# Starting the mixer and the dense layer on token tile 0, and reordering the heads' projection and the first loads, in a two-layer hybrid decoder trunk

## What is computed

```python
h = rmsnorm(x, pre_mix_g[l])
z = h @ w_in[l]                        # 2560 columns: q, k, v (8 heads x 64), u, g (512 each)
attn = dilated_mixture_attention(rotary(q), rotary(k), v)
uc = causal_dwconv(u, conv_w[l], conv_b[l])
rec = gelu(g) * rg_lru(uc, ...)        # two sigmoid gates, exp, sqrt, a scan over tokens
mixed = concatenate([rmsnorm(attn), rmsnorm(rec)])
x = x + rmsnorm(mixed @ w_out[l], post_mix_g[l])
h = rmsnorm(x, pre_ffn_g[l])
f = swiglu(h, ...) if l == 0 else moe_ffn(h, ...)   # dense 3584 wide; 8 experts, 2 per token
x = x + rmsnorm(f, post_ffn_g[l])
```

## Time and profile before

| | us |
|---|---|
| median of three executions | 1459.18 |
| the profiled execution | 1459.41 |
| its span, first to last instruction | 1457.6 |
| PE busy in the span | 1439.0 (fillers included) |
| DVE, ACT busy | 1196.2, 1032.0 |
| share of PE in the chain that ended last | 94% |
| start, mixer and norms of layer 0 | until about 128 |
| dense layer | 128 to 363 |
| second mixer and norms | 363 to 485 |
| router and experts | 485 to the end |

### The profile page before, as it was taken

One profiled execution on the slowest core, in us unless ns is written; L12 is line 12 of the kernel. 1 busy time (PEld: TensorE's weight loads), 2 busy tenths in 40 slices (PEclk: granted clock), 3 DMA queues, 4 the chain that ended last, 5 costly groups with the idle time before them and its releaser, 6 DMA issues.

```text
span 1457.6 us, 20750 instructions
## 1 busy us (share of the span) xinstructions
PE 1439.0 (99%) x7076; PEld 1193.5 (82%) x7076; DVE 1196.2 (82%) x1378; ACT 1032.0 (71%) x1258; POOL 14.5 (1%) x13
## 2 busy tenths in 40 slices
PE   8999999999999999999999999999999999999997
PEld 7887888888887688888888888888888888888885
DVE  7867656555776798898899899989889889989997
ACT  7665445445565677787797787788778779778774
POOL 0000000000000200000000000000000000001000
PEclk9999999999999999999999999999999999999999
DMA  9525874554433399999999999999999999999991
GB/s 367 208 100 197 339 274 177 201 200 173 147 143 127 112 423 409 361 393 388 378 370 397 375 362 409 376 353 400 386 358 399 388 366 378 397 373 372 420 400 65
DMA packets 68611, 454.11 MB, mean 312 GB/s; under 512 B 9424, under 2 KB 9552, under 8 KB 16592
## 3 DMA queue, kind: packets, MB, share of 16 engines
q1 hardware_dynamic: 60768, 432.47, 76.6%
q10 hardware_dynamic: 6640, 16.78, 3.2%
q0 software_dynamic: 1152, 4.19, 0.7%
HBM read 438.21 MB, written 15.20 MB: 311 GB/s over the span
## 4 chain that ended last, share of the span: by engine, by line
PE 94%; DVE 3%; ACT 2%; issue 1%; DMA 0%; DVEq 0%; ACTq 0%
PE psum L472 26%; PE psum L474 26%; PE psum L473 26%; PE psum L760 7%; PE psum L763 4%; PE psum L822 2%; ACT lru_b L938 1%; PE psum L479 1%; DVE hn L1300 1%; DVE xs L1322 1%; DVE hn L1316 1%; PE psum L621 0%; PE psum L561 0%; PE psum L805 0%; PE psum L499 0%
## 5 line engine op out<-in xcount | busy, mean ns | idle before, releaser
L1211 DVE TENSOR_TENSOR w_lo<-ring,w_hi 128x1024 fp32r<-128x1024 f32 x812 | 941.0, 1219 | 57.1 <-ACT w_hi L925 56.4
L925 ACT ACTIVATE w_hi<-ring 128x1024 fp32r<-128x1024 f32 x812 | 807.5, 1053 | 56.1 <-PE psum L474 49.7
L472 PE MATMUL psum<-w_hi,hT_both 128*128 128x512 f32 (+1 forms) x1088 | 424.4, 390 | 1.4 <-DVE hT_both L1222 1.4
L474 PE MATMUL psum<-w_hi,hT_both 128*128 128x512 f32 (+1 forms) x1088 | 417.6, 384 | 0.0
L473 PE MATMUL psum<-w_lo,hT_both 128*128 128x512 f32 (+1 forms) x1088 | 416.8, 383 | 0.0
L474 PEld LDWEIGHTS psum<-w_hi,hT_both 128*128 128x128 f32 x1088 | 204.4, 188 | 41.1
L472 PEld LDWEIGHTS psum<-w_hi,hT_both 128*128 128x128 f32 x1088 | 204.6, 188 | 40.7 <-DVE hT_both L1222 1.8
L473 PEld LDWEIGHTS psum<-w_lo,hT_both 128*128 128x128 f32 x1088 | 204.8, 188 | 38.4 <-issue 0.2
L472 PE MATMUL psum<-w_hi,act_hi 128*128 128x512 f32 x560 | 218.9, 391 | 0.9 <-DVE act_lo L1222 0.9
L474 PE MATMUL psum<-w_hi,act_lo 128*128 128x512 f32 x560 | 218.2, 390 | 0.0
L473 PE MATMUL psum<-w_lo,act_hi 128*128 128x512 f32 x560 | 218.2, 390 | 0.0
(11 more groups left out here) (236 smaller groups left out, 898.5 us busy)
## 6 DMA issues: line engine op xcount, KB each, us to landing
ring<-moe_gate SPq DMA_DIRECT2D x112, 1024.0 KB, 7.2
ring<-moe_up SPq DMA_DIRECT2D x112, 1024.0 KB, 7.6
ring<-moe_down SPq DMA_DIRECT2D x112, 1024.0 KB, 7.3
ring<-in_units SPq DMA_DIRECT2D x20, 1024.0 KB, 7.9
ring<-dense_gate SPq DMA_DIRECT2D x14, 1024.0 KB, 4.9
ring<-dense_up SPq DMA_DIRECT2D x14, 1024.0 KB, 4.8
ring<-dense_down SPq DMA_DIRECT2D x14, 1024.0 KB, 4.8
ring<-out_units SPq DMA_DIRECT2D x8, 1024.0 KB, 5.4
```

Source lines behind the costliest of these rows:

```text
L472: pe.matmul(dst, s_hi, m_hi, start=start, stop=False)
L474: return pe.matmul(dst, s_lo, m_hi, start=False, stop=stop)
L925: act.activation(w_hi[:, h % AHEAD, :], ring[:, n % RING, (h % 2) * HCOLS:(h % 2 + 1) * HCOLS], ACT.Copy).then_inc(hi_ready, 1)
L1211: dve.tensor_tensor(w_lo[:, h % AHEAD, :], ring[:, (h // 2) % RING, (h % 2) * HCOLS:(h % 2 + 1) * HCOLS], w_hi[:, h % AHEAD, :].bitcast(F3 ...
```

## The change

1. The order of units becomes: q and k of heads 0 to 3, then u, g, then q and k of heads 4 to 7, then v. Both copies of heads are read from banks 6 and 7.
2. In the second mixer and in the dense layer PE begins with tile 0's products as soon as hT of tile 0 is there, and turns tile 1 ahead of the last quarter of them. In the dense layer chunk 0's gate and up have the tokens as stationary factor and 256 weight columns moving, in place of both tiles' tokens moving; its product has tokens on the partitions and is turned by PE (turn_first_chunk) before act_hi and act_lo are made. Fillers at the norms are fewer (one for three in front, none behind in those two), two more at the start.
3. norm_lo of tile 0 stands ahead of update of tile 1 in every norm; a keep_up is moved into the norm ahead of the second mixer; at the last up the keep_up stands behind act_hi and act_lo; last_two finishes tile 0 before any piece of tile 1.
4. In the mixer: copy and rotation of heads 0 to 3 stand ahead of the sigmoids' product on DVE; copy, lo parts and rotation of heads 4 to 7 between scan and product with gelu; Square goes to lru_b and stands behind heads_hi(0) and a keep_up, ahead of values_out(0); the sums of squares move to head 4 of the loop; splits are moved.
5. At the start only the identity (128 columns of the constants) is loaded ahead of the units, the first unit in two halves, the parameters and other constants after it; ACT loads Sqrt's table before x is there.

The diff, cut to its core:

```diff
-IN_ORDER = [6, 7, 8, 9, 0, 1, 2, 3, 4, 5]
+IN_ORDER = [0, 1, 6, 7, 8, 9, 2, 3, 4, 5]
...
-            sync.dma_start(con[:, :], consts).then_inc(consts_loaded, 16)
-            sync.dma_start(par[:, :], params).then_inc(params_loaded, 16)
+            sync.dma_start(con[:, 0:P], consts[:, 0:P]).then_inc(ident_loaded, 16)
...
+                if n == 0:
+                    sync.dma_start(ring[:, 0, 0:HCOLS], src[:, 0:HCOLS]).then_inc(first_half_loaded, 16)
+                    sync.dma_start(ring[:, 0, HCOLS:UCOLS], src[:, HCOLS:UCOLS]).then_inc(unit_loaded[0], 16)
+                    sync.dma_start(par[:, :], params).then_inc(params_loaded, 16)
+                    sync.dma_start(con[:, P:NCON], consts[:, P:NCON]).then_inc(consts_loaded, 16)
...
+            def norm_head(n):
...
-                    warm(3, 6)
+                    warm(1, 6)
                 turn_rows_of(n, 0)
...
             def mixer(layer):
...
-                norm_transposes(layer, PRE_MIX)
-                channels(first, 0, layer)
-                channels(first + 1, 2)
-                channels(first + 2, 4)
-                channels(first + 3, 6)
+                norm_head(2 * layer)
+                if layer == 0:
+                    warm(2, 4)
+                    turn_rows_of(0, 1)
+                    warm(2, 4)
+                    for i in range(2):
+                        norm_wait(0, PRE_MIX, i, 1)
+                        for s in range(2):
+                            tokens(first + i, 6, i, s)
+                else:
+                    for i in range(2):
+                        norm_wait(layer, PRE_MIX, i, 0)
+                        for s in range(2):
+                            if i == 1 and s == 1:
+                                turn_rows_of(2 * layer, 1)
+                            tokens(first + i, 6, i, s, (0,))
+                    for i in range(2):
+                        norm_wait(layer, PRE_MIX, i, 1)
+                        for s in range(2):
+                            tokens(first + i, 6, i, s, (1,))
+                channels(first + 2, 0)
+                channels(first + 3, 2)
+                channels(first + 4, 4)
+                pe.wait_ge(qk_evac, 2 * layer + 1)
+                channels(first + 5, 6)
...
                 turn_heads(0, 0)
-                pe.wait_ge(rec2_ready, layer + 1)
-                pe.wait_ge(qk_evac, 2 * layer + 1)
-                for tt in range(TT):
-                    for j in range(LJ):
-                        mm = pe.matmul(ps[4][:, tt * EXPERTS:(tt + 1) * EXPERTS], lru_d[:, j, tt * P:(tt + 1) * P],
-                                       ones[:, 0:EXPERTS], start=(j == 0), stop=(j == LJ - 1))
-                mm.then_inc(ssR_ready, 1)
...
+                    if h == 4:
+                        squares()
...
                 piece(1, 0, 0)
                 piece(1, 1, 0)
-                piece(1, 0, 1).then_inc(half_done, 1)
                 piece(0, 0, 0)
                 piece(0, 1, 0).then_inc(tile0_done, 1)
+                piece(1, 0, 1).then_inc(half_done, 1)
...
+            def first_chunk():
+
+                n0 = PRE_AT[("gate", 0, 0)]
+                norm_head(1)
+                for tt in range(TT):
+                    for h in range(4):
+                        if h < 2:
+                            norm_wait(0, PRE_FFN, h, tt)
+                        if tt == 0:
+                            if h == 3:
+                                turn_rows_of(1, 1)
+                            pe.wait_ge(lo_ready, 2 * n0 + h + 1)
+                        s, bank = h % 2, (0 if h < 2 else 6)
+                        w = cols(half_at(2 * n0 + h), 0, FC, FC)
+                        for k in range(4):
+                            mm = product(ps[bank + tt][:, 0:FC], hT(4 * s + k, tt * P, (tt + 1) * P), w(k),
+                                         start=(s == 0 and k == 0), stop=(s == 1 and k == 3))
+                        if tt == TT - 1:
+                            mm.then_inc(half_done, 1)
...
+                    if kind == "gate" and c == 1:
+                        pe.wait_ge(silu_ready, 1)
+                    if kind == "up" and c == 1:
+                        turn_first_chunk()
...
             act.wait_ge(cleared, 1)
+            load_sqrt()
...
+                    if i == 0:
+                        keep_up(first + 5, AHEAD + 1)
...
-                keep_up(first + 5)
                 act.wait_ge(tanh_ready, LJ * (layer + 1))
                 act.activation(lru_a[:, :, :], lru_a[:, :, :], ACT.Sqrt).then_inc(sqrt_ready, 1)
                 keep_up(first + 6)
-                act.wait_ge(rec_ready, layer + 1)
-                act.activation(lru_d[:, :, :], lru_y[:, :, :], ACT.Square).then_inc(rec2_ready, 1)
                 keep_up(first + 7)
-                keep_up(first + 8)
...
                 heads_hi(0, 0)
+                keep_up(first + 8)
+                act.wait_ge(rec_ready, layer + 1)
+                act.activation(lru_b[:, :, :], lru_y[:, :, :], ACT.Square).then_inc(rec2_ready, 1)
                 values_out(0)
...
                 weighted(layer, which, 1)
+                norm_lo(n, 0)
                 update(layer, which, 1)
-                norm_lo(n, 0)
                 normalise(n, 1)
...
+                keep_up(first + 5, AHEAD + 1)
+                if layer == 0:
+                    dve.wait_ge(cs_ready, 1)
+                for tt in range(TT):
+                    rotate(layer, 0, tt)
...
                 link(ins)
+                heads_in(1)
+                heads_lo(0, 0)
+                for tt in range(TT):
+                    rotate(layer, 1, tt)
+                keep_up(first + 6)
                 dve.wait_ge(gelu_ready, 2 * (layer + 1))
                 dve.tensor_tensor(lru_y[:, :, :], lru_a[:, :, :], lru_g[:, :, :], ALU.mult).then_inc(rec_ready, 1)
...
+                    if h == 0:
+                        keep_up(first + 7)
...
+                    if h == 1:
+                        keep_up(first + 7, AHEAD + 1)
```

More of the change, by code:

```diff
@@ L533, in channels, with tokens @@
                     mm.then_inc(half_done, 1)
-            def tokens(n, bank, i, halves=(0, 1)):
-                for s in halves:
+            def tokens(n, bank, i, s, tiles=range(TT)):
+                if 0 in tiles:
                     pe.wait_ge(lo_ready, 2 * n + s + 1)
-                    w = cols(half_at(2 * n + s), 0, EC, EC)
-                    for tt in range(TT):
[L541 to L544, removed]
+                w = cols(half_at(2 * n + s), 0, EC, EC)
+                for tt in tiles:
+                    for k in range(2):
+                        kk = 4 * i + 2 * s + k
+                        mm = product(ps[bank + tt], hT(kk, tt * P, (tt + 1) * P), w(k),
+                                     start=(kk == 0), stop=(kk == DK - 1))
+                if TT - 1 in tiles:
                     mm.then_inc(half_done, 1)
@@ L563, in mixer @@
                     mm.then_inc(gates_mm, 1)
-                pe.wait_ge(gelu_ready, 2 * layer + 1)
-                for i in range(2):
-                    tokens(first + 4 + i, 4, i)
                 pe.wait_ge(gelu_ready, 2 * (layer + 1))
                 for i in range(2):
-                    tokens(first + 6 + i, 6, i)
+                    for s in range(2):
+                        tokens(first + 6 + i, 6, i, s)
                 def turn_heads(half, bank):
@@ L1107, in _ @@
                                   flat(lru_g).unsqueeze(1).to_broadcast([P, NEXTRA + 1, D])).then_inc(y_stored, 16)
-                if kind == "gate":
+                if (kind, c) == ("gate", 0):
+                    act.wait_ge(half_done, 2 * (n0 + 1))
+                    act.activation(silu[:, 0, :].rearrange("p (t f) -> p t f", t=TT), psum[:, 0:2, 0:FC],
+                                   ACT.Silu).then_inc(silu_ready, 1)
+                if kind == "gate" and c >= 1:
                     act.wait_ge(half_done, 2 * (n0 + n + 1))
-                    if c >= 1:
-                        act.wait_ge(silu_ready, c)
+                    act.wait_ge(silu_ready, c)
                     act.activation(gate_sum, psum[:, 0:2, T:2 * T], ACT.Copy).then_inc(gate_copied, 1)
-                if kind == "up":
+                if (kind, c) == ("gate", 1):
+                    act.wait_ge(prod0_tr, 1)
+                    act.activation(act_hi[:, 0:FPC, :], ps[2].rearrange("p (f t) -> p f t", f=FPC),
+                                   ACT.Copy).then_inc(act_hi_ready, 1)
+                if kind == "up" and c >= 1:
                     act.wait_ge(half_done, 2 * (n0 + n + 1))
@@ L1371, in mixer, with heads_in @@
                     softplus()
+                def heads_in(half):
+                    dve.wait_ge(half_done, 2 * (first + 2 + 6 * half))
+                    dve.tensor_copy(qk[:, :, half * AW:(half + 1) * AW], psum[:, 6:8, :]).then_inc(qk_evac, 1)
+                    dve.wait_ge(qk_evac, 2 * layer + half + 1)
```

(3 more changed lines are left out.)

148 lines of the change are left out of this document (78 added, 70 removed).

## The result

The changed kernel takes 1465.91 us (median of 5 executions, 1463.52 to 1468.28), the kernel before 1459.09 on the same chip (1459.04 to 1459.87): the ratio is 1.0045, 95% interval 1.0034 to 1.0055. It is slower by 6.8 us; the forecast was 1455.1, 4.1 us faster.

What follows compares the result with a forecast made beforehand. PE was taken as the bound, busy for 99% of the span. The terms -1.0 - 3.3 - 5.3 + 1.1 + 4.4 = -4.1 us gave 1455.1; own range 1453.3 to 1456.9, with rivals 1450.6 to 1457.8.

Steps and rivals of the forecast that it cites:

- the clock's term in the sum: Whole kernel: the sum of the five parts held no cost for falls of PE's granted clock.
- rival (c): Start, norms, mixers: clock falls to 0.50 at up to six waits, 1.7 us each; 1465.3 with all six; chance 0.08.
- The sign that I had set for being wrong: PE's granted clock at 0.50 anywhere from 16 us to the end of the last expert.
- Part 1: Dense layer: starting with tile 0 wins 3.8 us, turning the first product gives 0.5 back; minus 3.3.
- The silu: Dense layer, first chunk: ready at about 135.1, just as PE wants it; counted as nothing, ends 0 and 1.4 us.
- Part 2: Second mixer: splits moved behind act_hi and act_lo, then products start with tile 0; minus 5.3 us.
- Part 3: Norm ahead of the router: norm_lo of tile 0 ahead of update of tile 1 costs 1.1 us, ends 0 and 1.3.
- Part 4: Start: Sqrt's table loaded first and only the identity loaded early; products begin at 14.05, not 15.10; minus 1.0 us.
- Part 5: Both mixers' new order: waits for the values and at head 1 cost 2.2 us a layer, 4.4 in all.
- The wait for the values: Each mixer: PE, 22.8 us after the gate matmuls' start G, stands 1.5 us for ACT's copy; ends 0 and 2.5.
- The split at head 1: Each mixer: a DVE split of 1.14 us ahead of turned(1), 0.7 us of it not covered; ends 0 and 1.1.
- Rival (a): Mixers: the new waits are covered and PE never stands; sum -8.5 us, 1450.7; chance 0.25.

Runs made afterwards that it cites:

- e4: The kernel before with the fillers at its three later norms removed: 1466.68 us.
- e1: The changed kernel with filler matmuls added in PE's waits in both mixers, at tile 0's starts and at the router, nothing else: 1456.79 us.
- e7: e5 with the start on tile 0 undone ahead of the dense layer: both tiles turned before the first product, fillers in the wait: 1455.73 us.
- e8: e5 with the start on tile 0 undone ahead of the second mixer: both tiles turned before the first product, fillers in the wait: 1455.48 us.
- e11: e5 with five filler calls instead of six at the router's norm: 1450.18 us.
- e6: e5 but with norm_lo of tile 0 left ahead of update of tile 1 at the router's norm, as in the change: 1451.32 us.
- e12: e5 without the early load of Sqrt's table at the start: 1451.72 us.
- e2: The changed kernel with Square moved to head 1, behind the first copy of the values, no fillers added: 1455.29 us.
- e9: The changed kernel with two filler calls in the wait for the copy of the values in both mixers, nothing else: 1460.65 us.
- e10: The changed kernel with two filler calls ahead of the weighing of head 1 in both mixers, nothing else: 1458.47 us.
- e3: e2 without DVE's split at head 1: 1452.85 us.
- e5: e3 with norm_lo of tile 0 behind update of tile 1 again at the router's norm, and with e1's fillers at the norms: 1450.51 us.

## Why the prediction was wrong

**The step that failed is the clock's term in the sum, which was zero; the mechanism stood in rival (c).** I had named it there, with places and a price per fall, and gave it 0.08. The sign that I had set for being wrong, a granted clock of 0.50 anywhere from 16 us on, is what the trace shows. My reason against (c) was one row, 1.12 us of idle time at 371.12 without a fall. The new waits are longer: 1.2 us at the second mixer, 1.3 ahead of the weighing, 2.0 for the values in each mixer, and 2.3 at the router, which stands behind eight fillers as that row does. One wait without a fall says little about them. What I did not ask is what the fillers in those places did; e4 would have been the question. Four falls, one of 17 us, cost 9.1 us by the medians (1465.91 to 1456.79) and 11.5 in the profiled spans, the changed kernel's being its slowest execution (1466.4 to 1454.9). In the first mixer alone it is 7.8: the product behind the first wait starts 0.1 us earlier than in e1, the norm 7.7 later. Of the conditions of (c), six falls at 1.7 us, neither figure was right (four falls, 1.5 us for a short one, about 7.8 for the long one). That its 1465.3 comes close is luck: too many falls make up for a long one priced too low.

**Part 1, the dense layer: right.** From the last product of the out projection to gate 1 it is 16.8 us (127.72 to 144.51), before 20.6 (118.35 to 138.97): 3.8 won, as forecast, 0.4 of it given back where the first product is turned. e7 has 5.2 for the head start, as the steps do. The silu holds nobody: PE goes from the last quarter into gate 1 without a wait, and it does not wait at tile 1's turning either (0.2 us forecast).

**Part 2, the second mixer: right.** e8 has 5.0 for the start on tile 0, as the steps do. act_lo is there 3.7 us after the first piece (356.36 to 360.05), as forecast. From the last product of the dense layer to the end of the mixer's first four token halves e1 takes 16.4 us (360.73 to 377.18), the kernel before 21.7 (362.51 to 373.19, and 11.0): 5.2. The end of the dense layer itself, counted from its first piece, comes another 0.1 us earlier (11.98 for 12.12), which makes 5.4 for the 5.3 forecast (373.19 - 367.8, the forecast's own figures, is 5.4 too).

**Part 3, the router's norm: too small.** The hole is 10.86 us against 9.31, 1.55 instead of 1.1. The order of norm_lo is most of it: e11, with the old order and a filler that fits, is 1.1 us faster than e6, and its router starts 1.2 us earlier (476.03 for 477.23). The rest, 0.35, I did not trace.

**Part 4, the start: right.** Products begin at 13.75, forecast 14.05, before 15.10; 1.35 instead of 1.0. The half clock that stood there is gone. e12 puts 1.0 us of it down to the early load of Sqrt's table.

**Part 5, the mixers' order: the place right, the size short.** The wait for the values is 2.0 us, not 1.5: PE is at the wait when forecast, at G + 22.8, but ACT's Sqrt ends half a microsecond later than added up (G + 12.6 for G + 12.05, G being 408.76 here). The split at head 1 costs 0.7 as forecast. In e1, at full clock, the first mixer takes 106.25 us from its first to its last product (13.81 to 120.06), before 103.25 (15.10 to 118.35); the second, from the end of its first four token halves, 94.7 (377.18 to 471.90), before 91.9. Together 5.8 us for 4.4.

**The sum at full clock** is then -1.35 - 3.4 - 5.4 + 1.55 + 5.8 = -2.8 for the -4.1 forecast, and e1 measures -2.3 (medians) and -2.7 (spans). So of the miss of 10.8 us (1455.1 to 1465.91) 1.7 are terms of the sum (1455.1 to 1456.79), the other 9.1 the clock.

**Rival (a)** did not come true, and its figure doesn't fit its own condition: 1.5 us less in each mixer takes 3.0 from the sum, -7.1 and not -8.5, since the split at head 1 (0.7 a mixer) stays.

## What to carry to other kernels

Fillers are not waste to be trimmed after the rest: before taking one out, ask what the wait that it covers would cost with PE at half clock behind it. Give a new wait of PE as long as those that were followed by half clock here (1.2 us and more) a filler that ends just before the wait does. If executions of one kernel lie several microseconds apart where those of the kernel before agree, look at the granted clock first. In a queue written by hand, put an operation that waits (Square here) behind the ones that others wait for: that was worth 10.6 us (e2), more than either wait filled (5.3 in e9, 7.4 in e10).

## What the runs showed of the hardware

The waits that stood without a filler, and in which of the profiled executions PE was at half clock right behind them (one trace of each kernel):

| the wait | PE idle, us | bare in the traces of | half clock behind it in |
|---|---|---|---|
| first mixer, values | 1.87 | changed, e10 | e10 |
| first mixer, weighing of head 1 | 1.33 | changed, e2, e9 | all three |
| dense layer, tile 0's start | 1.21 | changed, e2, e3, e9, e10 | none |
| second mixer, tile 0's start | 1.20 | changed, e2, e3, e9, e10 | changed, e2 |
| second mixer, values | 1.87 | changed, e10 | changed |
| second mixer, weighing of head 1 | 1.33 | changed, e2, e9 | none |
| router, tile 1's turning | 2.32 | changed, e2, e3, e9, e10 | all but e10 |

- The length of the wait alone does not tell: 1.20 was followed by a fall where 1.87 (e10, second mixer) and 2.31 (e10, router) were not.
- The stretches seen at half clock were 3.41, 6.83, 10.24, 13.65 and 17.06 us long. In the longest PE was busy for 16.87 of 17.06 us and stayed at half clock; what ended it there, and after 3.41 us elsewhere, no run shows.
- Executions of one kernel lie 0.1 to 0.4 us apart where these waits have fillers or are gone (e1, e5 to e8, e11), and 2.4 to 4.8 apart where they are bare (the changed kernel, e2, e3, e9, e10). One or more stretches of 1.5 us each would make up such a difference; that is an estimate.
- Why one execution falls and another doesn't stays open: the runs only show that none fell with fillers in all of these waits.
